# Both gating products of a two-layer mixer kernel computed by a seven-product scheme

## The reference

```python
x = x + o @ w_out                        # end of the mixer, 1024 tokens x 1024
gate = sigmoid(x @ w_gate[m])            # 1024x1024 by 1024x1024: "the gating product"
x = x + gate * (p[m] @ w_up[m])          # p is 1024 x 256
```

## Time and profile before

| what | value |
|---|---|
| median of three runs | 2904.52 us |
| profiled execution: time, span | 2910.77 us, 2909.0 us |
| PE busy, share of the span | 2794.4 us, 96% |
| DVE, ACT, POOL busy | 1189.2 us, 904.1 us, 1022.1 us |
| mean granted TensorE clock | 0.98 of full speed |
| DMA | 155.56 MB, 53 GB/s |

### The profile page before, as it was taken

One profiled execution on the slowest core, in us unless ns is written; L12 is line 12 of the kernel. 1 busy time (PEld: TensorE's weight loads), 2 busy tenths in 40 slices (PEclk: granted clock), 3 DMA queues, 4 the chain that ended last, 5 costly groups with the idle time before them and its releaser, 6 DMA issues.

```text
span 2909.0 us, 41142 instructions
## 1 busy us (share of the span) xinstructions
PE 2794.4 (96%) x16908; PEld 2166.7 (74%) x16908; DVE 1189.2 (41%) x2813; ACT 904.1 (31%) x1701; POOL 1022.1 (35%) x447
## 2 busy tenths in 40 slices
PE   7979999899999999998999999999999999999998
PEld 5756676667777777776887878888888888887887
DVE  6998996556433333335335011111112121114423
ACT  5412233552334343335123222222222222224112
POOL 2532383133322222223542433333333333333631
PEclk8979899999999999999999999999999999999999
DMA  4100021031211111112211111111111111113211
GB/s 110 42 22 22 22 73 62 36 97 43 66 26 48 52 51 52 51 44 88 65 66 61 55 44 37 45 44 44 37 51 45 37 45 44 44 44 139 66 51 65
DMA packets 221334, 155.56 MB, mean 53 GB/s; under 512 B 25254, under 2 KB 207948, under 8 KB 221020
## 3 DMA queue, kind: packets, MB, share of 16 engines
q1 hardware_dynamic: 210076, 122.55, 14.6%
q10 hardware_dynamic: 11072, 30.39, 3.0%
HBM read 133.45 MB, written 19.47 MB: 53 GB/s over the span
## 4 chain that ended last, share of the span: by engine, by line
PE 51%; DVE 1%; issue 1%; ACT 1%; DMA 0%; ACTq 0%; DVEq 0%
PE proj L903 14%; PE proj L905 14%; PE proj L904 14%; PE out L1420 2%; PE score L1368 1%; PE score L1398 1%; PE score L1377 1%; PE proj L943 1%; PE out L904 0%; PE out L905 0%; PE out L903 0%; PE out L1387 0%; DMA y_scratch<-arena 0%; DVE arena L2332 0%; DVE arena L2459 0%
## 5 line engine op out<-in xcount | busy, mean ns | idle before, releaser
L903 PE MATMUL proj<-act_hi,w_hi 128*128 128x512 f32 x2560 | 1032.7, 403 | 13.2 <-ACT hT L1835 7.2
L905 PE MATMUL proj<-act_hi,w_lo 128*128 128x512 f32 x2560 | 1005.5, 393 | 0.0
L904 PE MATMUL proj<-act_lo,w_hi 128*128 128x512 f32 x2560 | 1005.0, 393 | 0.0
L776 POOL TENSOR_TENSOR w_hi<-w_raw,ones 128x1024 fp32r<-128x1024 f32 x175 | 419.7, 2398 | 1603.9 <-PE proj L905 1601.5
L903 PEld LDWEIGHTS proj<-act_hi,w_hi 128*128 128x128 f32 x2560 | 486.4, 190 | 127.2 <-issue 21.3
L905 PEld LDWEIGHTS proj<-act_hi,w_lo 128*128 128x128 f32 x2560 | 485.2, 190 | 104.8
L904 PEld LDWEIGHTS proj<-act_lo,w_hi 128*128 128x128 f32 x2560 | 486.0, 190 | 95.9 <-issue 0.2
L778 POOL TENSOR_TENSOR w_lo<-w_raw,w_hi 128x1024 fp32r<-128x1024 f32 x175 | 433.8, 2479 | 13.7
L1835 ACT ACTIVATE arena<-proj 128x512 f32<-128x512 f32 x236 | 176.0, 754 | 659.7 <-PE proj L905 635.7
L2459 DVE SCALAR_TENSOR_TENSOR arena<-arena,score 128x256 f32<-128x256 f32 (+1 forms) x192 | 76.1, 427 | 718.5 <-PE score L1368 676.8
L1861 ACT ACTIVATE arena<-score 128x512 f32<-128x512 f32 (+3 forms) x264 | 115.8, 487 | 195.5 <-PE score L1229 195.1
(11 more groups left out here) (268 smaller groups left out, 2881.5 us busy)
## 6 DMA issues: line engine op xcount, KB each, us to landing
w_raw<-dil_w_in_dram SPq DMA_DIRECT2D x80, 512.0 KB, 3.7
w_raw<-fox_w_in_dram SPq DMA_DIRECT2D x32, 512.0 KB, 4.2
w_raw<-w_in_dram SPq DMA_DIRECT2D x23, 512.0 KB, 3.9
y_scratch<-arena ACTq DMA_DIRECT2D x21, 512.0 KB, 3.6
act_lo<-y_scratch SPq DMA_DIRECT2D x21, 512.0 KB, 5.9
arena<-decay_scratch ACTq DMA_DIRECT2D x16, 512.0 KB, 5.7
w_raw<-ple_w_gate_dram SPq DMA_DIRECT2D x16, 512.0 KB, 3.7
arena<-x_dram SPq DMA_DIRECT2D x12, 512.0 KB, 5.3
```

The lines of the kernel that those rows point to most:

```text
L776: pool.tensor_tensor(hi, raw, one.unsqueeze(1).broadcast_to([P, KB, P]), ALU.mult).then_inc(w_hi_done, 1)
L903: pe.matmul(bank, hi, a_hi, start=first, stop=False)
L904: pe.matmul(bank, hi, a_lo, start=False, stop=False)
L905: return pe.matmul(bank, lo, a_hi, start=False, stop=last)
```

## The change

Each gating product is computed block-wise: tokens in two halves, contraction rows in two halves (A11, A12, A21, A22; first the token half, then the contraction half), output columns in two halves. Four times (r = 0 to 3) a pair of output tiles, r and r + 4, is made from seven products P1 to P7 in place of eight. Each product is 4 contraction tiles x 3 matmuls of 128x512 (`gate_product`). On the activation side four sums are needed: S1 = A21 + A22, S2 = S1 - A11, S3 = A11 - A21, S4 = A12 - S2, each of 4 tiles of 128x512. DVE forms them (`combine`) and they are split into hi (ACT) and lo (DVE) like the residual. On the weight side DVE forms four differences of weight quarters for each r in the raw weights' own places (`weight_turn`). POOL splits each of the seven weight quarters of 128x512 on its own (`gate_split`), into a ring of four places, and has taken over `p_lo`.

The seven products are added up in PSUM: P1 is put in bank a; ACT copies a to bank b (`onto`), then P2 goes on top of a (giving quarter 11) and P6 on top of b; ACT copies b to c, then P3 goes on top of b and P7 on top of c; P5 has a bank of its own that ACT copies to SBUF (`aside`), and DVE adds it (`joined`) for quarters 12 and 22; P4 goes on top of c (for r = 0 it has its own bank) for quarter 21. Sigmoid, multiplication and addition to `hT` are as before, per quarter. `up_quarter` replaces `up_half`.

Also: `arena` now starts ahead of `gains` and `small` in SBUF (before, 384 bytes of them lay ahead of it), and it is 16 columns wider. At the output's `turn_out` one tile rather than two comes ahead of the last `up`. The gate weights' loads are quarter loads on SP (`gate_weights`).

The core of the diff; the helpers `sigmoid`, `aside`, `combine`, `part_lo`, `weight_turn`, `joined`, `gated` and `squares` each issue one instruction, or one for each tile named, behind their waits:

```diff
+GATE_PAIRS = KB // 2
+GATE_MOVING = dict(P1="A11", P2="A12", P3="S4", P4="A22", P5="S1", P6="S2", P7="S3")
+GATE_QUARTERS = ("11", "12", "22", "21")
...
+def gate_order(r):
+
+    if r == 0:
+        return ("P1", "P2", "P4", "P6", "P5", "P7", "P3")
+    return ("P1", "P2", "P5", "P6", "P3", "P7", "P4") if r == 1 else ("P1", "P5", "P2", "P6", "P3", "P7", "P4")
...
-        gains = sb("gains", [P, 6, KB])
-        small = sb("small", [P, 48])
-        epsc = gains[:, 0, 0:1]
-        A_COLS = 22000
+        A_COLS = 22016
         with nc.sbuf_tensor("res_parts", [P, KB, 2, T], F32R) as res_parts, \
                 nc.sbuf_tensor("up_parts", [P, 2, 2, T], F32R) as up_parts:
             pass
         arena = sb("arena", [P, A_COLS])
+        gains = sb("gains", [P, 6, KB])
+        small = sb("small", [P, 40])
+        epsc = gains[:, 0, 0:1]
...
+        def gate_banks(r):
+
+            half = score[:, r % 2, 512:1024]
+            return dict(a=score[:, r % 2, 0:512], b=proj[0], c=half if r else proj[1], d=proj[1] if r else half, e=score[:, 1, 512:1024])
...
+            def p_lo(m, half):
+
+                tok = slice(half * 512, half * 512 + 512)
+                later(pool, PL[m], "ph", half + 1)
+                pool.tensor_tensor(act_lo[:, 0:2, tok], pT[:, half], act_hi[:, 0:2, tok].bitcast(F32), ALU.subtract)\
+                    .then_inc(PL[m]["pl"], 1)
...
+                    if name in ("P1", "P2", "P3"):
+                        kh, nu = dict(P1=(0, 0), P2=(1, 0), P3=(1, 1))[name]
+                        pool.wait_ge(gate_in[kh, nu], 16 * (XIN_LOADS + R + 1))
+                        raw = gate_raw(m, kh, nu)
+                    else:
+                        later(pool, PL[m], "turned", 4 * r + ("P7", "P5", "P6", "P4").index(name) + 1)
+                        raw = dict(P4=gate_raw(m, 1, 0), P5=gate_raw(m, 0, 1), P6=gate_raw(m, 0, 0), P7=w_turn3)[name]
+                    if n < 4:
+                        pool.wait_ge(pass_done[1], C_OUT[m] + 7 + n // 2)
+                    else:
+                        later(pool, PL[m], "used", n - 3)
+                    hi, lo = gate_ring(m, n)
+                    pool.tensor_tensor(hi, raw, ones[:, :].unsqueeze(1).broadcast_to([P, 4, P]), ALU.mult).then_inc(PL[m]["whi"], 1)
+                    later(pool, PL[m], "whi", n + 1)
+                    pool.tensor_tensor(lo, raw, hi.bitcast(F32), ALU.subtract).then_inc(PL[m]["wlo"], 1)
+                    if n in (1, 2):
+                        p_lo(m, n - 1)
...
+            def gate_product(m, r, name, ks=range(4), inside=None):
+
+                n = product_at(r, name)
+                if ks[0] == 0:
+                    later(pe, PL[m], "wlo", n + 1)
+                    if name == "P1":
+                        if r == 0:
+                            later(pe, PL[m], "ev", 2)
+                        elif r >= 2:
+                            later(pe, PL[m], "sig", quarter_at(r - 2, "11") + 1)
+                    if name in ("P2", "P6"):
+                        later(pe, PL[m], "onto", 2 * r + 1)
+                    if name in ("P3", "P7"):
+                        later(pe, PL[m], "onto", 2 * r + 2)
+                    if name == "P5" and r:
+                        if r == 1:
+                            later(pe, PL[m], "sum", sum_at(0, "21") + 1)
+                        else:
+                            later(pe, PL[m], "aside", max(copy_at(r - 1, "12"), copy_at(r - 1, "22")) + 1)
+                    if name == "P4" and r:
+                        later(pe, PL[m], "sum", sum_at(r, "22") + 1)
+                fresh = name in ("P1", "P5") or (name == "P4" and r == 0)
+                bank = gate_banks(r)[dict(P1="a", P2="a", P3="b", P6="b", P5="d", P7="c", P4="c" if r else "e")[name]]
+                hi, lo = gate_ring(m, n)
+                for k in ks:
+                    if r == 0:
+                        later(pe, PL[m], "lo", GATE_LO.index((GATE_MOVING[name], k)) + 1)
+                    if inside is not None and k == 3:
+                        inside()
+                    a_hi, a_lo = gate_part(GATE_MOVING[name], k)
+                    pe.matmul(bank, hi[:, k], a_hi, start=(fresh and k == 0), stop=False, skip_group_check=True)
+                    pe.matmul(bank, hi[:, k], a_lo, start=False, stop=False, skip_group_check=True)
+                    mm = pe.matmul(bank, lo[:, k], a_hi, start=False, stop=(k == 3), skip_group_check=True)
+                if ks[-1] == 3:
+                    mm.then_inc(PL[m]["used"], 1)
...
-                for j in range(KB - 1):
-                    for half in range(2):
-                        gate_half(m, j, half)
-                        up_half(m, j, half)
-                gate_half(m, KB - 1, 0)
-                up_half(m, KB - 1, 0)
+                gate_product(m, 0, "P1")
+                up_quarter(m, 0, "11")
+                gate_product(m, 0, "P2")
+                gate_product(m, 0, "P4")
+                up_quarter(m, 0, "22")
+                gate_product(m, 0, "P6")
+                gate_product(m, 0, "P5")
+                gate_product(m, 0, "P7")
+                gate_product(m, 0, "P3")
+                for r in range(1, GATE_PAIRS):
+                    gate_product(m, r, "P1")
+                    if r == 1:
+                        up_quarter(m, 0, "12")
+                        up_quarter(m, 0, "21")
+                        gate_product(m, r, "P2")
+                        up_quarter(m, r, "11")
+                        gate_product(m, r, "P5")
+                    else:
+                        gate_product(m, r, "P5")
+                        gate_product(m, r, "P2")
+                        up_quarter(m, r, "11")
+                    gate_product(m, r, "P6")
+                    up_quarter(m, r, "12")
+                    gate_product(m, r, "P3")
+                    gate_product(m, r, "P7")
+                    up_quarter(m, r, "22")
+                    if r < GATE_PAIRS - 1:
+                        gate_product(m, r, "P4")
+                        up_quarter(m, r, "21")
...
-            gate_half(1, KB - 1, 1, part=0)
-            token_sums(ND, 0, (dacc,), 2 * (KB - 2) + 1)
-            gate_half(1, KB - 1, 1, part=1, inside=lambda: spread_rows(ND, 0, ((0, 36),)))
-            up_half(1, KB - 1, 1)
+            gate_product(1, GATE_PAIRS - 1, "P4", ks=range(0, 2))
+            token_sums(ND, 0, (dacc,), GATE_SQUARES.index((7, 0)) - 1)
+            gate_product(1, GATE_PAIRS - 1, "P4", ks=range(2, 4), inside=lambda: spread_rows(ND, 0, ((0, 28),)))
+            up_quarter(1, GATE_PAIRS - 1, "21")
+            later(pe, PL[1], "aside", copy_at(GATE_PAIRS - 1, "12") + 1)
+            later(pe, PL[1], "sum", sum_at(GATE_PAIRS - 1, "22") + 1)
...
+                for j in range(4):
+                    residual_hi(m, "A11", j)
+                    combined_hi(m, j, "S3", j)
+                p_turned(m, 0)
+                residual_hi(m, "A12", 0)
+                p_turned(m, 1)
+                residual_hi(m, "A22", 0)
+                residual_hi(m, "A12", 1)
+                residual_hi(m, "A22", 1)
+                residual_hi(m, "A12", 2)
+                residual_hi(m, "A12", 3)
+                later(act, PL[m], "ev", 2)
+                p_hi(m, 0)
+                later(act, PL[m], "pl", 1)
+                residual_hi(m, "A22", 2)
+                def combined(k):
+                    for x in range(3):
+                        combined_hi(m, 4 + 3 * k + x, ("S1", "S2", "S4")[x], k)
+
+                combined(0)
+                p_hi(m, 1)
+                combined(1)
+                onto(m, 0, "P1")
+                later(act, PL[m], "pl", 2)
+                residual_hi(m, "A22", 3)
+                combined(2)
+                combined(3)
...
+            def onto(m, r, name):
+
+                banks = gate_banks(r)
+                later(act, PL[m], "used", product_at(r, name) + 1)
+                if name == "P1":
+                    if r == 0:
+                        act.wait_ge(pass_free[0], C_OUT[m] + KB)
+                    else:
+                        later(act, PL[m], "sum", sum_at(r - 1, "12") + 1)
+                    act.activation(banks["b"], banks["a"], ACT.Copy).then_inc(PL[m]["onto"], 1)
+                else:
+                    if r == 0:
+                        act.wait_ge(pass_free[1], C_OUT[m] + KB)
+                    elif r <= 2:
+                        later(act, PL[m], "aside", copy_at(0, "21") + 1)
+                    else:
+                        later(act, PL[m], "sig", quarter_at(1, "21") + 1)
+                    act.activation(banks["c"], banks["b"], ACT.Copy).then_inc(PL[m]["onto"], 1)
...
+            def first_gates(m):
+
+                sigmoid(m, 0, "11")
+                onto(m, 0, "P6")
+                aside(m, 0, "12")
+                aside(m, 0, "22")
+                sigmoid(m, 0, "12")
+                sigmoid(m, 0, "22")
+                aside(m, 0, "21")
```

(62 more changed lines are left out.)

385 lines of the change are left out of this document (252 added, 133 removed).

## The result

The changed kernel takes 2943.32 us, the median of four runs (2940.11 to 2945.67), against 2904.28 us for the kernel before in the same comparison: a ratio of 1.0129, 95% interval 1.0109 to 1.0149. A second set of runs gave 1.0115 (1.0098 to 1.0132). It is slower by 32 to 43 us by the first interval and by 28.5 to 38 by the second; 29.9 were predicted. The profiled execution took 2941.60 us, with a span of 2939.8.

What follows compares the result with a forecast made beforehand. PE bounds the kernel, by matmul count and distance. m = 1 +16.6, m = 2 +7.9 and clock +5.4 give +29.9 on a span of 2909.0: 2938.9, or 2940.7 profiled; median 2934 us, range 2912 to 2952.

Steps and rivals of the forecast that it cites:

- The matmuls, -14.0 us a gate: Gate stages: 480 matmuls at 0.2331 us become 432 at 0.2265, so 14.0 us less each, 28.0 in all.
- The gate's start, +22.8 us: r = 0 and start of r = 1: PE waits of 10.3, 4.6, 4.6 and 3.3 us in each gate.
- The seam: From m = 1's gate into dil: waits of 15.3 us against 8.0 before; +7.8 with 1.0 in r = 3, less 0.5.
- The end of m = 2: Before the last up: one tile transposed in place of two saves 0.9 us.
- leaves alone: After DVE's first output scaling: 14 us of DVE and store work remain that the change does not touch.
- The clock, +5.4 us: PE at half clock after waits: three times 1.8 us, once in each gate behind r = 0, once in the seam.
- Rival D: After PE's waits: clock stays at half for 10 us, some 15 us more, 2949; chance 0.12.
- A: The forecast itself: waits as summed, 2934, by itself 2922 to 2947; chance 0.70.
- The argument against D: At the gate's start: P6 waits for DVE anyway, so slow matmuls before it cost nothing; 3.4 us sufficed at 1575.
- The chain that ends at t = 0.6: Gate's start, from -5.2: DVE residual 0.69, ACT 0.63 and 1.06, POOL p_lo 2.4, ACT hi part of A22 0.63.
- B: Gates: POOL's quarter splits slip between DVE's instructions, waits 11.7 us a gate, seam unchanged, about 2905; chance 0.13.
- C: Gate's start: bank copy in time, P2(0) starts before about t = 5, only up 21's 4.6 us stay, 2885; chance 0.05.

Runs made afterwards that it cites:

- both arena experiments: Kernel before with arena ahead of the small tensors: ratio 0.9985; changed kernel with the small tensors ahead of arena again: gate of m = 1 2.3 to 2.6 us longer.
- the last version: Kernel before with arena first, one tile transposed ahead of m = 2's last up, new order at the seam of m = 1: 2899.45 us, ratio 0.9966.

## Why the prediction was right, and where it was short

The sign and the mechanism are right; the size was 29.9 us, the stretches give 22.2 + 12.7 = 34.9, and the differences of the medians 32.5 and 39.

- **The matmuls, -14.0 us a gate: right.** 0.2267 us apart, not 0.2331, and both arena experiments tie that to where the arena starts.
- **The gate's start, +22.8 us: right in sum.** Without a wait P2(1) would start 120 x 0.2267 = 27.2 us behind P1. It starts at 50.5 and 51.8, so 23.3 and 24.6 late. P2(0) started at 14.5 (14.4 was said), by two errors of which one hid the other: the exclusion of DVE and POOL cost 6.2 us ahead of P2 and not 5.3, and without it P2 would start at 8.3 and not 9.0. P6(0)'s wait ended at 27.9 (27.8), since DVE sets that moment, but it was 1.88 us long and not 4.6: P2's twelve matmuls at half clock took the rest. Up 21 waited 4.18 (4.6), P2(1) 1.90, with the slow matmuls ahead of it (3.3). Without POOL's splits the start was 41.6 and not 39. The later start of the gate of m = 2 goes with 3.4 us at half clock behind P6(0)'s wait; with the waits filled it is 50.9.
- **The seam: the waits right, the total short.** Token sums 5.08 (5.4), spread 0.43 behind a root that ran meanwhile (2.3), second lo part 4.26 (4.7). From where PE ran dry, 121.8 us behind P1, to the last matmul of dil's first two tiles is 44.5 us. The steps as put give 15.3 + 108 x 0.2267 + 1.3 = 41.1; the clock is to be added.
- **The end of m = 2: the -0.9 us is right, "leaves alone" is not.** In the last version the same step took 126.53 to 125.70. But from DVE's first scaling to the end the changed kernel takes 15.26 us and the one before 14.16: these 1.1 us, which go with an instruction load among the stores, are a term that the forecast put at nothing.
- **The clock, +5.4 us: this is the term that was mis-sized.** I took three stretches of 1.8 us each. There are seven in the gates and the seam, five of them 10.2 us long. Where they cost is behind P2(1). From there to where PE ran dry, 300 matmuls or 68.0 us, gate 1 took 71.4; 1.0 was put for it, 1.6 are the 3.3 us that end at 1504.61 at half speed, and 0.8 are small gaps. In the gate of m = 2, what follows P2(1) took 90.5 us; the steps give 87.5, and the difference is the 1.1 of the stores and 3.6 us at half speed. And at the seam the stretch of 10.2 us cost 2.4 us more than one of 3.4 did with the same waits, where 1.8 was put for all of it. The kernel with all waits filled is 5.6 us shorter without the stores, and has 10 us at half clock left in the seam, worth at most 5 more. To close the sum the clock would have to be 5.4 + 5.0 - 1.1 = 9.3 us, which lies between 5.6 and 10.7; it isn't measured by itself. Rival D had the length (half for 10 us behind the waits) but not the price, 15 us; the truth lies between A and D. The argument against D, that slow matmuls ahead of a wait for DVE cost nothing, holds behind P2(0) only.
- **Two sums that are off.** The chain that ends at t = 0.6 adds up to 0.2 (DVE's lo part started at 0.4), and B's 28 - 23.4 + 0.9 is 5.5 and not 4 or 5. Neither moves the forecast.
- **Rivals B and C fell.** POOL's quarters don't slip between DVE's instructions, and the bank copy, even when it comes early, only hands the wait to P4 and P6.

The part not settled: why one wait of 5.6 us is followed by 3.4 us at half clock and another by 10.2. The runs show both, and nothing that I changed on purpose chose between them. A forecast of such a seam is uncertain by 2.4 us for this alone.

## What to carry to other kernels

When PE is the bound and has no gaps, count a scheme that saves matmuls in the currency of the engines that must prepare it: here 48 matmuls a gate, 11 us, were saved for 23 to 25 us at its start. Nine to ten of these go when POOL's splits are made small, as they and the sums on DVE exclude each other at the one place where nothing covers them; the other 14 to 15 remain even then. Price each new PE wait with the slow matmuls behind it, and when a wait is taken away look at the next instruction that DVE holds up. And compare starts of matmuls with the same shapes in different tensors: a distance that differs by 3% may be a matter of where a tensor lies.

## What the runs showed of the hardware

- Matmuls of 128x512 in this format start 0.2267 us apart when both SBUF operands lie in tensors that start on a 512-byte step, counted from the first tensor. With `arena` 384 bytes off it is 0.2334 within products with the moving operand in it and 0.2335 within those with only the stationary one (0.2331 over all 449); with 352 bytes it is 0.2342 and 0.2323, and 0.2276 for products of the same kernel with neither. Other offsets weren't tried.
- The half-clock stretches around PE's waits of 4 to 10 us lasted 3.4 to 13.7 us by the trace, and two kernels with the same wait had different ones (5.55 and 5.61 us, then 3.4 and 10.2). With the waits of both gates filled with unused matmuls the clock was 1.00 through both.
- A 16 KB packet of the queue that loads instructions fell among the output's eight stores in nine of fourteen traces, and these nine took 0.65 to 1.55 us longer from the first scaled tile to the end. No run sets the packet apart as the cause.
- An ACT copy from one PSUM bank to another takes 0.58 us.
- A DVE instruction of 128x8 with two SBUF inputs, 0.17 us alone, took 1.25 us beside a POOL split: what it pays is the rest of POOL's instruction, not a share of its own length.
